# Two pairs of weight loads moved three places back in the SyncE queue of a two-block transformer kernel

## The reference

```python
u = rms_norm(h, norm_mix_pre[l])
(q_n, kc_n, vc_n, ks_n, vs_n, kw_n, vw_n, g_n,
 q_s, k_s, v_s, gate_a, gate_b) = jnp.split(u @ w_in[l], IN_OFFSETS, axis=-1)
kc = compress_kv(kvr(kc_n), cmp_pos_k[l], cmp_w1_k[l], cmp_w2_k[l])
vc = compress_kv(kvr(vc_n), cmp_pos_v[l], cmp_w1_v[l], cmp_w2_v[l])
# compress_kv: blocks of 32 tokens, flattened to 2048, then
#   jax.nn.gelu(flat @ w1) @ w2      with w1 of 2048 x 256
```

## Time and profile before

| | |
|---|---|
| timed runs | 1335.89, 1338.89, 1338.92 us; median 1338.89 us |
| profiled execution | 1336.42 us, its span 1334.4 us |
| TensorE busy | 1289.5 us, 97% of the span |
| VectorE, ScalarE busy | 920.4 us (69%), 653.0 us (49%) |
| granted TensorE clock, mean | 0.993 of full |
| moved by DMA | 317.96 MB, 238 GB/s on average |

### The profile page before, as it was taken

One profiled execution on the slowest core, in us unless ns is written; L12 is line 12 of the kernel. 1 busy time (PEld: TensorE's weight loads), 2 busy tenths in 40 slices (PEclk: granted clock), 3 DMA queues, 4 the chain that ended last, 5 costly groups with the idle time before them and its releaser, 6 DMA issues.

```text
span 1334.4 us, 16031 instructions
## 1 busy us (share of the span) xinstructions
PE 1289.5 (97%) x6423; PEld 1056.2 (79%) x6423; DVE 920.4 (69%) x1028; ACT 653.0 (49%) x923; POOL 28.1 (2%) x54
## 2 busy tenths in 40 slices
PE   8898898999999999999999999999999999999998
PEld 8876577887887788887788887787888887788887
DVE  6237887877768776677866667966766786744444
ACT  5256756544456333345534445753333566644442
POOL 2200010000000000000000000000000000000000
PEclk9999998999999999999999999999999999999999
DMA  9975588888875888874777884688778633455551
GB/s 294 282 219 154 154 294 323 320 332 294 308 262 196 285 299 283 284 252 142 270 262 279 280 310 142 200 286 283 265 275 289 211 127 102 151 190 189 189 189 63
DMA packets 162761, 317.96 MB, mean 238 GB/s; under 512 B 7128, under 2 KB 108944, under 8 KB 153472
## 3 DMA queue, kind: packets, MB, share of 16 engines
q1 hardware_dynamic: 158800, 305.44, 66.4%
q0 software_dynamic: 3712, 11.45, 3.3%
q10 hardware_dynamic: 176, 0.05, 0.0%
HBM read 314.56 MB, written 1.84 MB: 237 GB/s over the span
## 4 chain that ended last, share of the span: by engine, by line
PE 84%; DVE 8%; ACT 3%; DMA 3%; issue 1%; SPq 1%; ACTq 0%; DVEq 0%
PE bank L745 26%; PE bank L747 26%; PE bank L746 26%; DMA raw<-in_w_in 3%; PE bank L858 2%; DVE full L2002 2%; DVE wlo L1893 1%; DVE xt L1990 1%; DVE mix L1988 1%; ACT whi L1418 1%; PE bank L1133 1%; PE bank L782 1%; PE bank L806 1%; ACT mix L1434 0%; SPq L585 0%
## 5 line engine op out<-in xcount | busy, mean ns | idle before, releaser
L1893 DVE TENSOR_TENSOR wlo<-raw,whi 128x2048 fp32r<-128x2048 f32 x198 | 453.4, 2291 | 231.9 <-ACT whi L1418 231.7
L1418 ACT ACTIVATE whi<-raw 128x2048 fp32r<-128x2048 f32 x201 | 384.6, 1914 | 198.1 <-PE bank L747 168.6
L745 PE MATMUL bank<-whi,uhi 128*128 128x512 f32 (+2 forms) x1152 | 450.3, 391 | 13.2 <-DVE ulo L2015 7.5
L747 PE MATMUL bank<-whi,ulo 128*128 128x512 f32 (+2 forms) x1152 | 441.8, 384 | 0.0
L746 PE MATMUL bank<-wlo,uhi 128*128 128x512 f32 (+2 forms) x1152 | 441.0, 383 | 0.0
L745 PEld LDWEIGHTS bank<-whi,uhi 128*128 128x128 f32 x1152 | 217.8, 189 | 60.0 <-issue 17.2
L747 PEld LDWEIGHTS bank<-whi,ulo 128*128 128x128 f32 x1152 | 217.4, 189 | 43.1
L746 PEld LDWEIGHTS bank<-wlo,uhi 128*128 128x128 f32 x1152 | 217.9, 189 | 39.7 <-issue 0.2
L745 PE MATMUL bank<-whi,hsplit 128*128 128x512 f32 x480 | 189.8, 396 | 0.0
L747 PE MATMUL bank<-whi,hsplit 128*128 128x512 f32 x480 | 187.1, 390 | 0.0
L746 PE MATMUL bank<-wlo,hsplit 128*128 128x512 f32 x480 | 186.9, 389 | 0.0
(11 more groups left out here) (280 smaller groups left out, 930.4 us busy)
## 6 DMA issues: line engine op xcount, KB each, us to landing
raw<-in_ffn_w_in SPq DMA_DIRECT2D x176, 512.0 KB, 4.7
ada<-in_ada_w SPq DMA_DIRECT2D x72, 1024.0 KB, 7.0
raw<-in_ffn_w_out SPq DMA_DIRECT2D x44, 1024.0 KB, 5.2
raw<-in_w_in SPq DMA_DIRECT2D x16, 1024.0 KB, 10.6
raw<-in_w_mlp_in SPq DMA_DIRECT2D x16, 1024.0 KB, 6.8
raw<-in_w_mlp_out SPq DMA_DIRECT2D x16, 1024.0 KB, 5.2
ada<-in_kv_ada_w SPq DMA_DIRECT2D x8, 1024.0 KB, 7.3
raw<-in_w_kv SPq DMA_DIRECT2D x8, 1024.0 KB, 5.1
```

What stands on the lines that cost most here:

```text
L745: nc.tensor.matmul(o, sh, mh, start=start, stop=False, skip_group_check=skip)
L747: return nc.tensor.matmul(o, sl, mh, start=False, stop=stop, skip_group_check=skip)
L1418: ins = nc.scalar.activation(whi[:, ring(n), :], raw[:, ring(n), :], ACT.Copy)
L1893: ins = nc.vector.tensor_tensor(wlo[:, ring(n), :], raw[:, ring(n), :], whi[:, ring(n), :].bitcast(F32), ALU.subtract)
```

## The change

The loads of the compressed branch's first-layer weights change places in SyncE's queue. Before, the pair for keys was issued ahead of slot 5 and the pair for values ahead of slot 7. Now the pair for keys is issued behind slot 6 and the pair for values behind slot 7. Buffers, sizes, counters and the wait for `u_turned` stay, and so does every instruction of the other engines.

```diff
--- before.py
+++ after.py
@@ -577,12 +577,6 @@
                 sp.dma_start(xt[:, t, :], A["x"][0, t * P:(t + 1) * P, :]).then_inc(x_in[t], 16)
             w1 = [A[name][0].rearrange("(s k p) c -> s p k c", p=P, k=8) for name in ("cmp_w1_k", "cmp_w1_v")]
             for n in range(8):
-                if n in (5, 7):
-                    a = (n - 5) // 2
-                    if a:
-                        sp.wait_ge(u_turned, 4)
-                    for h in range(2):
-                        sp.dma_start(w1s[a][h].rearrange("p (k c) -> p k c", k=8), w1[a][h]).then_inc(w1_in[a], 16)
                 if n in QUERY_SLOTS:
                     c0, q = QUERY_SLOTS[n]
                     slot(n, v4, w_in[:, 4 * q:4 * q + 4, c0:c0 + 512])
@@ -590,6 +584,12 @@
                     slot(n, v8, w_in[:, :, starts[n]:starts[n] + 256])
                 if n == 2:
                     sp.dma_start(cst[:, P:CST["cos"][0]], cst_dram[:, P:CST["cos"][0]]).then_inc(cst_rest, 16)
+                if n >= 6:
+                    a = n - 6
+                    if a:
+                        sp.wait_ge(u_turned, 4)
+                    for h in range(2):
+                        sp.dma_start(w1s[a][h].rearrange("p (k c) -> p k c", k=8), w1[a][h]).then_inc(w1_in[a], 16)
             for n in range(8):
                 c0 = q2_ + 512 * (n // 2)
                 slot(G + n, v4, w_in[:, 4 * (n % 2):4 * (n % 2) + 4, c0:c0 + 512])
```

## The result

The median after is 1344.66 us (1343.51 to 1345.75, 5 runs) against 1338.92 us before (1335.89 to 1342.51, 5 runs): ratio 1.0039, interval 1.0021 to 1.0057, so 5.7 us slower. The forecast was +5.5 us and 1343.0 us. The profiled executions differ by more, 1345.02 against 1336.42 us, because the one of before lies at the fast end of its scatter; experiment 5 comes back to this.

What follows compares the result with a forecast made beforehand. TensorE bounds the whole span, but the opening is bound by transfers until gate slot G2 lands. 3.2 us for an idle DMA queue plus 2.3 us for the lower clock gave +5.5 us on 1337.5: 1343.0 us, range 1335 to 1347.5.

Steps and rivals of the forecast that it cites:

- Step 1, the hole: DMA queue runs dry from 29.1 to 32.3 us while SP waits to issue slot 6: 3.2 us, bounds 0.6 and 3.9.
- Step 2, slot 7 at 54 us: Slot 6 lands at 36.7 us, slot 7 at 54.1 us, 3.3 us sooner; TensorE's 5.77 us wait falls to about 2.5.
- Step 3, what is late next: Gate slots behind the value pair: G0 at 68.1 us, G2 at 78.7 to 78.9 us (+3.2 us); TensorE idle 9.9 us.
- Step 4, the clock: TensorE's long run starts at the lower clock after its stand: about 2.3 us, bounds 0 and 2.6.
- The sum: Whole kernel: 3.2 + 2.3 = +5.5 us, nothing absorbed after 79 us; median 1343.0 us.
- (a): A lagging ring fills the DMA gap, loss 0.6 us plus the clock: +2.9 us, 1340.4 us; chance 0.15.
- (b): At TensorE's restart the lower clock is not the price thought: +3.2 us, 1340.7 us; chance 0.06.
- (c): Early slot 7 releases G2's issue 3.3 us earlier, G2 lands at 72.4 us: -3.2 us, 1334.3 us; chance 0.15.
- (d): Load order does nothing, early slots 5 to 7 and late key weights cancel: 0 us, 1337.5 us; chance 0.08.

Runs made afterwards that it cites:

- experiment 5: The kernel before, unchanged, profiled twice more: 1336.05 us and 1340.78 us.
- Experiments 2 and 3: Only key pair moved behind slot 6, 1345.92 us; kernel after with key pair ahead of slot 6, 1340.72 us, or with VectorE converting slot 3 earlier, 1340.84 us.
- experiment 3's first order: Kernel after, but with the key pair behind slot 5 and ahead of slot 6: median 1340.72 us, ratio 1.0004 to before.
- experiment 1: Kernel before with only the value pair moved behind slot 7: median 1340.47 us, ratio 1.0007.
- experiment 6: ScalarE's copies put ahead of its conversions of G1 and G2: 1332.52 us with only the value pair moved, 1338.65 us on after, 1335.11 us on before.
- experiment 4: Kernel after plus 50 extra TensorE transposes ahead of its wait for ScalarE's copy: median 1342.91 us, ratio 1.0025 to before.
- the fastest variant: Kernel before with only the value pair moved behind slot 7 and ScalarE's copies ahead of converting G1 and G2: median 1332.52 us, ratio 0.9957.

## Why the prediction was right, and where its terms were off

The forecast held in sign and cause, and in size at the medians; the terms did less well than their sum.

- **Step 1, the hole**: its place was right (29.1 to 32.3 us forecast; empty from 30 to 32 us, thin on either side). Its price was not. I took 3.2 us with 3.9 as the upper bound; TensorE's restart in the profiled execution is 5.55 us late. Two parts are missing. The edges are wider than I had them: the 1.5 MB lacking from 28 to 33 us are 4.1 us at the 372 GB/s of before. And the flow is thin behind the hole, 226 GB/s for five microseconds against 316, which adds 1.4 us; I had let it come back at its full rate. Both figures are estimates from those windows. The thin flow stands in all four traces with the hole (226, 229, 233 and 233 GB/s) and in none of the other eight (316 to 381 GB/s). Experiments 2 and 3 show that the hole is the cause: with it +5.7 and +6.4 us by the medians, without it +1.0 to +1.5, whichever way it is filled. By the medians of after and of experiment 3's first order the hole costs 3.9 us, by their ratios 4.7.
- **Step 2, slot 7 at 54 us**: wrong. Slot 6 landed at 40.78 us, not 36.7, and slot 7 at 57.16 us. The lone slot's 5.3 us didn't carry over to slot 6, which had the next loads right behind it and took 9.4 us; which of the two, the company or the thin flow, did it wasn't tested. TensorE's first stand remained (5.51 us) with its lower clock (0.50 at 60 to 62 us). It didn't matter for the end, since the copy was later still; the slot's early landing of experiment 1 shows the gain would have been spent anyway.
- **Step 3, what is late next**: right in kind, not in its pieces. G0 was forecast for 68.1 us and came at 74.72, and G2 followed it in 6.5 us where I had kept the 10.6 us of before, so two misses of opposite sign left G2 at 81.25 us, 2.4 us behind the 78.7 to 78.9 us forecast. TensorE waited for a copy behind late gate slots, 7.06 us instead of 9.9, as it was done later. That the copy hangs on G2 only by ScalarE's order is shown by experiment 6.
- **Step 4, the clock**: 2.3 us taken, 3.05 and 3.1 us measured (kcT in after, and in experiment 4). It was my upper bound that was too tight (2.6), for the lower clock lasted here from 80 to 90 us, 6.5 us of it behind the restart, and I had reckoned with 5.2 us of work at that level.
- **The sum**: 5.5 us against 5.7 in the medians and 8.6 in the profiled pair. In the profiled pair both terms are larger than mine; the medians differ by less, and the likely reason is that before pays the clock in part of its executions. I had met the scatter of 1335.9 to 1338.9 us with a mean and no reason. That 5.5 met 5.7 is therefore luck: two terms that were too small, against a baseline that seems to hold part of the second already.
- **Rivals**: (a), a filled hole, is refuted by the share of 0.00; (b) by experiment 4; (c), the early slot 7 that wins, by experiment 1, though experiment 6 shows that it wins once ScalarE's order lets it; (d) by the result.

Left open: why the flow is thin for five microseconds behind the hole, why the medians give the clock less than the traces do, and where the slower executions of the fastest variant lose their time.

## What to carry to other kernels

A load that nobody waits for yet can still be the one that keeps the DMA engines busy: before moving it behind a load that has to wait, look whether anything is left in the queue during that wait. In a stage bound by transfers, ask of each early landing what in the waiting engine's program stands between it and its user; here reordering copies on ScalarE won time, and no order of loads alone did. And price a stand of TensorE with the clock behind it: a stand that is short enough in one execution may not be in the next.

## What the hardware showed that I had not expected

Behind a stretch of 1 to 2 us with next to nothing in flight the DMA engines moved 226 to 233 GB/s from 33 to 38 us, at a share of 0.90 to 0.94, in each of four traces; in the eight traces without that hole they moved 316 to 381 GB/s in the same window. And the kernel before, unchanged, was caught in both conditions on one core: 1336 us in two executions with the clock up at the start of its long run, 1340.8 us in a third with the clock down, parted by 2.0 us in the start of G2's conversion (75.32 and 77.32 us).
